# Values times probabilities in two passes: high and low value columns side by side as the stationary operand

## The reference

```
p = jax.nn.softmax(s, axis=-1)                      # layer 0, per head
o = jnp.einsum('bhqk,bhkd->bhqd', p, vt)            # head dim d = 64
...
p = (e / denom)                                     # layer 1, per head
o = jnp.einsum('bhgnqs,bnshd->bnqhgd', p, vb)
return o @ w_out                                    # both
```

## Time and profile before

| | |
|---|---|
| Device time, median of 3 runs | 1278.08 us (1276.99 to 1278.34) |
| Span of the profiled execution | 1274.1 us |
| Time of the profiled execution outside its span | not shown by the profile; the runs' median lies 4.0 us above the span |
| TensorE busy | 1187.7 us (93%), 5545 matmuls |
| VectorE busy | 696.6 us (55%) |
| ScalarE busy | 528.4 us (41%) |
| Mean granted TensorE clock | 0.980 of full speed |
| The fox loop from its first value product on | 78 to 272 us |
| The swa loop | 735 to 850 us |

### The profile page before, as it was taken

One profiled execution on the slowest core, in us unless ns is written; L12 is line 12 of the kernel. 1 busy time (PEld: TensorE's weight loads), 2 busy tenths in 40 slices (PEclk: granted clock), 3 DMA queues, 4 the chain that ended last, 5 costly groups with the idle time before them and its releaser, 6 DMA issues.

```text
span 1274.1 us, 15424 instructions
## 1 busy us (share of the span) xinstructions
PE 1187.7 (93%) x5545; PEld 970.8 (76%) x5545; DVE 696.6 (55%) x1014; ACT 528.4 (41%) x947; POOL 100.5 (8%) x201
## 2 busy tenths in 40 slices
PE   5999999997999999999995889798799999999998
PEld 3778888775688888888883668676588888888887
DVE  3777777755864223444337778854864322444333
ACT  3455555633453212333223678853444211333212
POOL 4111111000300000000002013200300000000000
PEclk8999999999999999999998989999899999999999
DMA  6333333212143333333331133313133333333312
GB/s 142 86 84 75 86 74 84 67 53 80 34 116 106 108 90 92 99 99 99 95 90 29 50 83 99 84 34 99 33 100 113 101 99 89 93 99 100 99 49 66
DMA packets 205605, 107.63 MB, mean 84 GB/s; under 512 B 13777, under 2 KB 201169, under 8 KB 205553
## 3 DMA queue, kind: packets, MB, share of 16 engines
q1 hardware_dynamic: 190960, 98.05, 26.5%
q0 software_dynamic: 6096, 8.86, 3.2%
q10 hardware_dynamic: 8496, 0.04, 0.4%
HBM read 96.38 MB, written 2.16 MB: 77 GB/s over the span
## 4 chain that ended last, share of the span: by engine, by line
PE 78%; DVE 12%; ACT 7%; issue 2%; ACTq 1%; DVEq 0%
PE acc L492 14%; PE acc L493 14%; PE acc L494 14%; PE logit L494 9%; PE logit L493 9%; PE logit L492 9%; PE mix L627 3%; ACT yT L1124 2%; DVE h_lo L1237 2%; DVE tmp L1226 2%; DVE w_lo L1198 1%; PE trans L603 1%; DVE xT L1232 1%; ACTq L915 1%; DVE pt_lo L1324 1%
## 5 line engine op out<-in xcount | busy, mean ns | idle before, releaser
L1198 DVE TENSOR_TENSOR w_lo<-w_raw,w_hi 128x1024 fp32r<-128x1024 f32 x179 | 219.3, 1225 | 191.2 <-ACT w_hi L866 187.4
L866 ACT ACTIVATE w_hi<-w_raw 128x1024 fp32r<-128x1024 f32 x179 | 187.8, 1050 | 197.1 <-PE acc L494 93.9
L492 PE MATMUL acc<-h_hi,w_hi 128*128 128x512 f32 x536 | 223.7, 417 | 35.7 <-DVE h_lo L1237 32.9
L493 PE MATMUL acc<-h_lo,w_hi 128*128 128x512 f32 x536 | 212.6, 397 | 0.0
L494 PE MATMUL acc<-h_hi,w_lo 128*128 128x512 f32 x536 | 212.0, 395 | 0.0
L492 PEld LDWEIGHTS acc<-h_hi,w_hi 128*128 128x128 f32 x536 | 102.7, 192 | 68.3 <-DVE h_lo L1237 44.7
L492 PE MATMUL acc<-act,w_hi 128*128 128x512 f32 x384 | 150.8, 393 | 1.5 <-DVE act L1336 1.3
L494 PE MATMUL acc<-act,w_lo 128*128 128x512 f32 x384 | 149.6, 390 | 0.0
L493 PE MATMUL acc<-act,w_hi 128*128 128x512 f32 x384 | 149.5, 389 | 0.0
L494 PEld LDWEIGHTS acc<-h_hi,w_lo 128*128 128x128 f32 x536 | 102.5, 191 | 23.0
L1040 ACT ACTIVATE act<-tmp 128x512 f32 (+1 forms) x64 | 40.5, 633 | 189.7 <-DVE tmp L1425 189.7
(11 more groups left out here) (219 smaller groups left out, 1734.8 us busy)
## 6 DMA issues: line engine op xcount, KB each, us to landing
w_raw<-in_mlp_w_up_dram SPq DMA_DIRECT2D x64, 512.0 KB, 4.0
w_raw<-in_mlp_w_down_dram SPq DMA_DIRECT2D x64, 512.0 KB, 3.6
w_raw<-in_fox_w_in_dram SPq DMA_DIRECT2D x25, 512.0 KB, 3.8
act<-act POOLq DMA_DIRECT2D x52, 128.0 KB, 2.5
w_raw<-in_swa_w_in_dram SPq DMA_DIRECT2D x10, 512.0 KB, 4.0
w_raw<-in_fox_w_out_dram SPq DMA_DIRECT2D x8, 512.0 KB, 3.6
w_raw<-in_swa_w_out_dram SPq DMA_DIRECT2D x8, 512.0 KB, 4.1
yT<-in_x_dram SPq DMA_DIRECT2D x4, 512.0 KB, 6.6
```

Of the source, the lines that this page charges most:

```text
L492: nc.tensor.matmul(a[:, :], w_hi[:, s, k, :], rhs_hi(k), start=first and k == 0, stop=False)
L493: nc.tensor.matmul(a[:, :], w_hi[:, s, k, :], rhs_lo(k), start=False, stop=False)
L866: nc.scalar.activation(w_hi[:, n % RING, :, :], w_raw[:, n % RAW, :, :], ACT.Copy).then_inc(whi_done, 1)
L1198: nc.vector.tensor_tensor(w_lo[:, n % RING, :, :], w_raw[:, n % RAW, :, :], f32(w_hi[:, n % RING, :, :]), ALU.subtract).then_inc(wlo_done, 1)
```

## The change

The two value buffers become one, `v_parts`, of 256 columns for each key block: high of side 0, low of side 0, low of side 1, high of side 1, each 64 wide. The stationary operand of a head is its own 128 columns, high and low side by side. Two passes, with the high and with the low probabilities, then give four partial products: the high values' sum in one half of the PSUM rows and the low values' in the other. Afterwards the halves are added: ScalarE copies one half of a head's bank to the rows of `o_sum` (`part_o`), VectorE adds the other half there (`add_o`), which frees the bank (`mix_free`). When both heads of a pair are in `o_sum`, ScalarE copies all 128 rows to `o_hi` (`high_o`) and VectorE subtracts (`low_o`); from then on `o_done` counts pairs. `o_sum` is the buffer `sq_sum`, which the attention stages do not use otherwise. `high_v` and `low_v` become two instructions of 128x256 each.

```diff
-        v_hi = sb("v_hi", [P, 2, NB, P], F32R)
-        v_lo = sb("v_lo", [P, 2, NB, P], F32R)
+        v_parts = sb("v_parts", [P, 2, NB, 2 * P], F32R)
...
+        o_sum = sq_sum
...
+        def v_both(slot, b, side):
+            return v_parts[:, slot, b, P * side:P * side + P]
+
+        def v_high(slot):
+            return [v_parts[:, slot, :, 3 * HD * side:3 * HD * side + HD] for side in range(2)]
+
+        def v_low(slot):
+            return v_parts[:, slot, :, HD:3 * HD]
...
                 if hd >= 2:
-                    pe.wait_ge(o_done, hd - 1)
+                    pe.wait_ge(mix_free, hd - 1)
...
-                    for v, t in ((v_hi, pt_hi), (v_hi, pt_lo), (v_lo, pt_hi)):
-                        mm = nc.tensor.matmul(o[:, kb * P:SEQ], v[:, p % 2, kb, :], t[:, pt],
-                                              start=(kb == 0 and v is v_hi and t is pt_hi),
-                                              stop=(kb == NB - 1 and v is v_lo))
+                    for t in (pt_hi, pt_lo):
+                        mm = nc.tensor.matmul(o[:, kb * P:SEQ], v_both(p % 2, kb, hd % 2), t[:, pt],
+                                              start=(kb == 0 and t is pt_hi), stop=(kb == NB - 1 and t is pt_lo))
...
-                pe.wait_ge(o_done, heads0 + 2 * k + 2)
+                pe.wait_ge(o_done, heads0 // 2 + k + 1)
...
             def high_v(j, slot):
                 sc.wait_ge(t_ready, j + 1)
-                nc.scalar.activation(v_hi[:, slot, :, :].rearrange("p b n -> p (b n)"), trans[j % 2][:, :],
-                                     ACT.Copy).then_inc(vh_done, 1)
+                src = trans[j % 2][:, :].rearrange("p (b n) -> p b n", b=NB)
+                for side, to in enumerate(v_high(slot)):
+                    last = nc.scalar.activation(to, src[:, :, half(side)], ACT.Copy)
+                last.then_inc(vh_done, 1)
...
-            def high_o(hd, rows):
-
-                p, side = divmod(hd % HEADS, 2)
+            def part_o(hd):
+
+                side = hd % 2
                 sc.wait_ge(pv_done, hd + 1)
-                nc.scalar.activation(o_hi[half(side), p, :], mix[hd % 2][rows, :], ACT.Copy).then_inc(oh_done, 1)
+                if hd >= 2:
+                    sc.wait_ge(o_done, hd // 2)
+                nc.scalar.activation(o_sum[half(side), :], mix[hd % 2][half(1 - side), :],
+                                     ACT.Copy).then_inc(part_done, 1)
+
+            def high_o(pair):
+
+                sc.wait_ge(mix_free, 2 * pair + 2)
+                nc.scalar.activation(o_hi[:, pair % PAIRS, :], o_sum[:, :], ACT.Copy).then_inc(oh_done, 1)
...
                 if h >= 1:
-                    high_o(h - 1, half((h - 1) % 2))
+                    part_o(h - 1)
...
                 if nxt:
                     fox_exp(h + 1, 1)
+                if even and h >= 2:
+                    high_o(h // 2 - 1)
                 if even and proj:
                     split(t + RING)
...
-            high_o(HEADS - 1, half(1))
+            part_o(HEADS - 1)
+            high_o(PAIRS - 1)
...
                 if nxt:
                     swa_exp(h + 1, 1)
+                if even and h >= 2:
+                    high_o(PAIRS + h // 2 - 1)
                 swa_high_t(h, 1)
...
-            def low_o(hd, rows):
-                p, side = divmod(hd % HEADS, 2)
-                ve.wait_ge(oh_done, hd + 1)
-                nc.vector.tensor_tensor(o_lo[half(side), p, :], mix[hd % 2][rows, :], f32(o_hi[half(side), p, :]),
+            def add_o(hd):
+                rows = half(hd % 2)
+                ve.wait_ge(part_done, hd + 1)
+                nc.vector.tensor_tensor(o_sum[rows, :], mix[hd % 2][rows, :], o_sum[rows, :],
+                                        ALU.add).then_inc(mix_free, 1)
+
+            def low_o(pair):
+                ve.wait_ge(oh_done, pair + 1)
+                nc.vector.tensor_tensor(o_lo[:, pair % PAIRS, :], o_sum[:, :], f32(o_hi[:, pair % PAIRS, :]),
                                         ALU.subtract).then_inc(o_done, 1)
...
                 if h >= 1:
-                    low_o(h - 1, half((h - 1) % 2))
+                    add_o(h - 1)
...
                 fox_low_t(h, 1)
+                if even and h >= 2:
+                    low_o(h // 2 - 1)
                 if nxt:
                     fox_max(h + 1, 3)
...
                 swa_low_t(h, 0)
                 swa_low_t(h, 1)
+                if even and h >= 2:
+                    low_o(PAIRS + h // 2 - 1)
                 if nxt:
                     swa_norm(h + 1)
```

More of the change, by code:

```diff
@@ L697, in out_proj @@
                     finish(project(w0 + o, g0 + o, of(o_hi), of(o_lo), EARLY if o < 2 else 0, KT, rhs_ready=(
[L698 removed]
+                        lambda k: pe.wait_ge(o_done, heads0 // 2 + k + 1)) if o == 0 else None))
                 post_stat(norm)
@@ L796, in swa_mix @@
                     n = P * min(2, NB - kb)
[L797 to L800, removed]
+                    for t in (pt_hi, pt_lo):
+                        mm = nc.tensor.matmul(o[:, kb * P:kb * P + n], v_both(0, kb, hd // GROUP),
+                                              t[:, kb * 2 * P:kb * 2 * P + n], start=(kb == 0 and t is pt_hi),
+                                              skip_group_check=True, stop=(kb == NB - 1 and t is pt_lo))
                 mm.then_inc(pv_done, 1)
@@ L1160, in _ @@
                 if h >= 1:
-                    high_o(HEADS + h - 1, half((h - 1) // GROUP))
+                    part_o(HEADS + h - 1)
                 if not even and rotates:
@@ L1171, in _ @@
                     swa_high_k(1)
-            high_o(2 * HEADS - 1, half(1))
+            part_o(2 * HEADS - 1)
+            high_o(2 * PAIRS - 1)
             out_proj(1, W_SWA_OUT, G_SWA_OUT, 5)
@@ L1316, in low_v @@
                 ve.wait_ge(vh_done, i + 1)
-                nc.vector.tensor_tensor(v_lo[:, slot, :, :].rearrange("p b n -> p (b n)"), trans[j % 2][:, :],
-                                        f32(v_hi[:, slot, :, :].rearrange("p b n -> p (b n)")),
-                                        ALU.subtract).then_inc(t_free, 1)
+                src = trans[j % 2][:, :].rearrange("p (b n) -> p b n", b=NB)
+                for side, high in enumerate(v_high(slot)):
+                    last = nc.vector.tensor_tensor(v_low(slot)[:, :, half(side)], src[:, :, half(side)], f32(high),
+                                                   ALU.subtract)
+                last.then_inc(t_free, 1)
             def low_t(i, j, at, n):
@@ L1555, in _ @@
                     angles(p + 1)
-            low_o(HEADS - 1, half(1))
+            add_o(HEADS - 1)
+            low_o(PAIRS - 1)
             out_proj(W_FOX_OUT, G_FOX_OUT, 1)
@@ L1604, in _ @@
                 if h >= 1:
-                    low_o(HEADS + h - 1, half((h - 1) // GROUP))
+                    add_o(HEADS + h - 1)
                 if not even and rotates:
@@ L1615, in _ @@
                     split(W_SWA + 4 + p + RING)
-            low_o(2 * HEADS - 1, half(1))
+            add_o(2 * HEADS - 1)
+            low_o(2 * PAIRS - 1)
             out_proj(W_SWA_OUT, G_SWA_OUT, 5)
```

4 lines of the change are left out of this document (3 added, 1 removed).

## The result

The changed kernel takes 1284.9 us, median of 4 runs (1282.62 to 1285.91), beside 1277.62 for the kernel before (4 runs, 1276.99 to 1278.34). The ratio is 1.0057, 95% interval 1.0045 to 1.0068. The profiled execution took 1284.11 us with a span of 1282.1, 8.0 more than before.

The account below looks back on a forecast made before the run. The prediction took a chain between ScalarE and VectorE to bound both attention loops. Fox -1.85 and swa +7.5 gave +5.6 us, from 1278.1 to 1283.7; its own range was 1282 to 1286, the 8-in-10 range 1276 to 1287.

Parts of the forecast that it names:

- The copy: ScalarE's added 128x512 copy per pair, high_o: 0.54 us, from 0.52 to 0.63, on the chain in both loops.
- The subtraction: VectorE's added 128x512 subtraction per pair, low_o: 0.65 us, from 0.61 to 0.69; hidden in fox, on the chain in swa.
- The values in halves: high_v and low_v as two instructions each: 0.3 us together, counted once, at h = 14 of fox.
- Fox, six periods: Head 0's to head 12's product: each period -0.1 to -0.15 us, the one before head 10 some 0.5 beside; together -1.2.
- From head 12 to the end of fox: Head 12's product -0.65 us, values +0.3, head 13 0, heads 14 and 15 -1.3, the end +1.3.
- Rival 4: Clock falls behind fox's new waits of some 1.2 us, costing some 1.5 a pair, +9, 1293 us; chance 0.05.
- Swa, h = 2 to 12: Both added pair instructions on the chain: six times 1.19 us, +7.1; none of the 0.47 saved per head counts.
- Per head nothing: Both loops: part_o and add_o each replace another instruction, so they add nothing per head.
- The ends: End of each loop: high_o and low_o add +1.3 us in full; TensorE waits 2.0 instead of 0.67.
- The first: TensorE is the path in both loops, so the saving counts: -14.2 us, 1264; chance 0.06.
- the second: Fox has unseen slack, so the even product is not held: 6.6 us more gained, -1.0, 1277; chance 0.12.
- the third: Swa hides the pair's two instructions because an earlier step held by TensorE comes sooner: -1.5 us, 1276.5; chance 0.06.

Follow-up runs that it names:

- e5: The kernel before with the third pass of the value product left out and nothing in its place; 1270.64 us, ratio 0.9948.
- e10: e3 with VectorE doing fox_scale and the third row maximum ahead of the weight split in fox's even iterations; 1267.99 us, ratio 0.9928.
- e6: The changed kernel with a second VectorE subtraction like low_o in fox's even iterations; 1285.53 us, ratio 1.0072.
- e1: The changed kernel with fox's high_o moved from ahead of the weight split to behind the second transposed quarter's high part; 1280.36 us, ratio 1.0034.
- e7: The changed kernel with eight unused 512-column matmuls filling TensorE's 2.47 us wait in iteration 13 of fox; 1284.79 us, ratio 1.0059.
- e4: The changed kernel with a second sum buffer in swa, so part_o has one wait instead of two; 1285.2 us, ratio 1.0064.
- e2: The changed kernel with swa's high_o moved ahead of the scaling and low_o into the next odd iteration behind its first maximum; 1278.9 us, ratio 1.0013.
- e3: The changed kernel with both the fox move of e1 and the swa moves of e2; 1274.05 us, ratio 0.9977.
- e11: e3 with the two early output projections taking the seventh row block of both tiles before the eighth of either; 1272.73 us, ratio 0.9965.

## Why the prediction was right

The forecast was +5.6, from 4.4 to 7.5; the medians differ by 7.3 and the spans by 8.0, which is beyond 7.5. The mechanism held: both loops are bound by the chain between ScalarE and VectorE, the copy and the subtraction cost what they were put at where they stand on it, and what TensorE saves becomes waiting. That the number came so close owes something to luck. The sum has a slip of 0.3, swa lost 0.9 us by a step that was put at nothing, and 1.4 us of the traces' difference is the clock.

- **What bounds the kernel.** Right in both loops, and e5 is the direct test: a third of the value product taken out for nothing gives 6.4 of 17.9 us, and nothing from head 1 to head 13 of swa. (The product that the prediction calls head 9's, at 816.46 in swa, is head 10's; the reading of its wait holds.) TensorE is at 93% over the span, and yet the order of a few instructions on VectorE, at 55%, was worth 6.1 us (e10). The Trainium skill, page Perfetto Trace Analysis, section Identifying the Most-Contended Engine, would optimize the engine of the highest occupancy first, and judges TensorE's headroom by its weight loads rather than its matmuls. Weight loads are busy 76% here, still the highest share, and in these two loops the runs disagree with the rule.
- **The prices.** The copy was put at 0.54 and costs 0.52. The subtraction was put at 0.65 and costs 0.60 in swa and nothing in fox (e6), as foreseen. The values in halves were put at 0.3 together: the two copies are drawn 0.66 us long for 0.60, the two subtractions 0.74 for 0.68, so some 0.1.
- **Fox, six periods.** Forecast -1.2, measured -0.98 (160.27 to 159.29 us from head 0's to head 12's product). e1 shows that 0.52 a pair was the copy's place. The wait that the even product kept was named in advance as 1 to 1.2 us, and is 1.08 to 1.16 but for head 10.
- **From head 12 to the end of fox.** Forecast -0.35, measured +0.92. Head 14 to head 15 is -0.65 and head 15 to the output projection +0.76, which is the lost 0.65 of product and +1.4 for the pair: both as worked out. The stretch from head 12 to head 14 is off: +0.81 where -0.35 was due. That is the clock of this execution, not the term. Over 244 to 256 us it is 0.72 for 0.86 before (the stretches under e7). The other traces whose fox is the changed kernel's agree: 22.29 us at 0.72 here, 22.23 at 0.72 in e4, 20.86 at 0.86 in e2. At the clock of the kernel before, with its 21.48, the stretch would be -0.62. So 1.43 us of the 8.0 comes from how the clock fell in the two executions traced. Rival 4 had this fall behind the waits of some 1.2 us; there it did not happen in any period from head 2 to head 12, and the clock of 78 to 272 us is 0.98.
- **Swa, h = 2 to 12.** Forecast +7.1 (six times 1.19), measured +7.56: six pairs of +1.41, +1.40, +1.42, +1.12, +1.11 and +1.10. The last three are the 0.52 and 0.60. The first three have 0.3 more each, which lies in the odd iteration. The prediction had put a head's own instructions at nothing ("Per head nothing"), and `part_o`, the one of these four instructions that the change replaced, was not free here. It is on ScalarE, and e3, which has the pair's instructions elsewhere, keeps it:

```profile
775.10 1.06 ACT L877 ACTIVATE w_hi<-w_raw 128x1024 fp32r<-128x1024 f32 x1
776.19 0.60 ACT L994 ACTIVATE sq_sum<-mix 64x512 f32<-64x512 f32 x1
776.68 0.62 ACT L1130 ACTIVATE act<-yT 128x512 fp32r<-128x512 f32 x1
777.33 0.60 ACT L983 ACTIVATE pt_hi<-trans 128x512 fp32r<-128x512 f32 x1
```

These starts are 1.09, 0.49 and 0.65 apart. In the kernel before the same four instructions of h = 7 start at 790.39, 791.34, 791.81 and 792.33 (the last two are the earlier trace rows), 0.95, 0.47 and 0.52 apart: 0.29 less. The durations agree to 0.02 or so; what is gone is the overlap. This is no accident of one trace. In all eleven kernels with `part_o` these steps are the long ones at h = 3, 5, 7 and 9; in the two with the old copy, the kernel before and e5, they are long at h = 9 alone (804.49 to 806.71 before), so the fourth pair shows no difference. It isn't the added wait (e4). What it is in `part_o`, and why h = 9 loses the overlap with the old copy too, stays open.
- **The ends.** The waits were forecast at 2.0 and are 2.04 and 2.05. TensorE's wait at swa's transposes was to grow by half a microsecond and grew by 1.1: the forecast counted the shorter product there and not the subtraction's 0.60. At the end of swa, from head 13 on, +0.44 was measured for +0.4.
- **The rivals.** The first, that TensorE is the path and the time falls to 1264, is out by e5. The second, slack in fox, is out by the waits ahead of the even products, and the third, that swa hides the pair, by the 0.51 and 0.60. The fourth, a fall of the clock behind the even products' waits, did not come.
- **The sum itself.** It has a slip: fox's terms as listed (-1.2, -0.65, +0.3, -1.3, +1.3) add up to -1.55, and -1.85 leaves out the 0.3 for the values. So the terms said +5.95. To that come 1.27 from head 12 to the end of fox (1.43 by the clock, less 0.16), 0.46 in swa's pairs, 0.22 in fox's periods, 0.04 at the end of swa, and 0.30 at the starts of the two loops, which no term had: 0.14 in fox, most of it there before the loop, and 0.16 in swa, where h = 1 loses the same overlap. That is 8.24. The stretches between the attentions and behind the second take 0.24 less, which gives the 8.0 of the spans.

## What to carry to other kernels

Fewer matmuls on an engine at 93% can make a kernel slower: ask for each stretch which wait ends last, and take the work out alone (e5) before paying for its removal. In swa two instructions of 0.52 and 0.60 us cost 6.35 us over six pairs of heads where they stood ahead of what another engine waits for, and nothing a few places further on, so an instruction that nobody awaits soon goes behind those that somebody does. When a chain between two engines sets the period, look for an instruction in it that only fills a buffer for later: here taking the weight split from ahead of a maximum was worth 6.1 us, nearly as much as the third pass left out for nothing (6.4). And before a step of 1 or 2 us between two traces is put down to a change, the granted clock of that stretch is to be compared.

## What the runs showed of the hardware

- Where TensorE's clock falls differs between traces of the same instructions. At h = 13 it fell to 1.2 GHz behind a wait of 2.47 us (granted clock 0.72 and 0.50 in the changed kernel). With that wait filled it stayed up, and fell behind a later one, of 2.05 us (0.73 and 0.85 in e7). e11, with the same wait at h = 13 (2.46), kept the full clock there and behind its waits at the end of fox. The distance between the products of heads 13 and 14 was 12.74 us in the changed kernel, 11.27 in e3 and 10.59 in e11, and in traces with the changed kernel's own fox instructions 12.74 and 12.69 (e4) at a clock of 0.72 over 244 to 256 us, and 11.32 (e2) at 0.86. In the sum it hardly showed: the mean granted clock of all these executions lies between 0.973 and 0.980.
- The start of an instruction on ScalarE behind a 128x1024 copy was 0.95 or 1.09 us after it, with nearly the same durations. Which of the two it was went with the kernel: at h = 3, 5 and 7 of swa 1.07 to 1.09 in all eleven kernels with `part_o` behind it, 0.95 in the two with the old copy, and 1.07 to 1.09 in all thirteen at h = 9. What decides it is open.
